# Turning raw rows of x first and normalising them afterwards in a hybrid decoder step

## What is computed

```python
def rms_norm(x, g):
    xf = x.astype(jnp.float32)
    y = xf * lax.rsqrt(jnp.mean(xf * xf, axis=-1, keepdims=True) + NORM_EPS)
    return (y * g.astype(jnp.float32)).astype(x.dtype)

hn   = rms_norm(x, norm_mix_g)              # both groups of tokens
proj = hn @ w_in                            # z, xbc, dt, u5, gates
...                                         # SSD branch, S5 branch from u5, merge
mn   = rms_norm(mem_prompt, norm_mem_kv_g)  # 256 memory tokens
k, v = mn @ w_mem_k, mn @ w_mem_v
...                                         # cross-attention, hierarchical MoE, final norm
```

## Time and profile before

| what | value |
|---|---|
| median of three executions | 1179.93 us (1176.68 to 1180.23) |
| profiled execution, device time | 1180.31 us |
| its span | 1178.6 us |
| PE busy | 980.5 us (83%) |
| DVE busy | 458.9 us (39%) |
| ACT busy | 302.5 us (26%) |
| mean DMA rate | 253 GB/s |
| mean granted TensorE clock | 0.923 of full speed |

### The profile page before, as it was taken

One profiled execution on the slowest core, in us unless ns is written; L12 is line 12 of the kernel. 1 busy time (PEld: TensorE's weight loads), 2 busy tenths in 40 slices (PEclk: granted clock), 3 DMA queues, 4 the chain that ended last, 5 costly groups with the idle time before them and its releaser, 6 DMA issues.

```text
span 1178.6 us, 15892 instructions
## 1 busy us (share of the span) xinstructions
PE 980.5 (83%) x6486; PEld 657.4 (56%) x6486; DVE 458.9 (39%) x854; ACT 302.5 (26%) x608; POOL 53.1 (5%) x78
## 2 busy tenths in 40 slices
PE   3999999999999999999898989666767677755664
PEld 2778567986669999999767953222222222221111
DVE  3998956304667554545554241010011001100113
ACT  4142124225446434534343331000000000000002
POOL 1602200000110000000000000000000000000000
PEclk9999999999999999999999969778888888888888
DMA  9482434013636374523588328999999999999991
GB/s 275 99 202 81 155 117 143 2 40 84 195 92 232 139 290 143 188 85 131 199 305 332 149 107 361 421 421 421 422 420 421 421 422 421 422 421 421 421 421 63
DMA packets 90691, 297.69 MB, mean 253 GB/s; under 512 B 20973, under 2 KB 30921, under 8 KB 65916
## 3 DMA queue, kind: packets, MB, share of 16 engines
q1 hardware_dynamic: 87844, 288.25, 63.8%
q0 software_dynamic: 2256, 7.80, 1.9%
q10 hardware_dynamic: 520, 0.62, 0.2%
HBM read 286.76 MB, written 9.90 MB: 252 GB/s over the span
## 4 chain that ended last, share of the span: by engine, by line
issue 69%; PE 5%; DMA 1%; ACT 0%; POOL 0%; DVE 0%; SPq 0%; POOLq 0%
PE bank L1537 1%; PE bank L1582 1%; DMA ring<-in_state_ssd_dram 1%; PE bank L1265 1%; PE bank L1589 1%; PE bank L1568 0%; PE bank L1546 0%; ACT ops L977 0%; PE bank L1523 0%; PE bank L1593 0%; ACT usplit L969 0%; PE bank L1577 0%; ACT ring L983 0%; POOL out_ssdp_dram L729 0%; DVE ring L2279 0%
## 5 line engine op out<-in xcount | busy, mean ns | idle before, releaser
L1879 PE MATMUL bank<-ring,work 128*32 128x512 f32 x768 | 154.4, 755 | 43.1 <-DMA work<-in_w_exp_up_dram 16.2
L1879 PE MATMUL bank<-work 128*32 128x512 f32 x256 | 115.4, 768 | 37.7 <-DMA ring<-in_w_exp_up_dram 20.9
L1280 PE MATMUL bank<-work,ring 128*128 128x320 f32 (+1 forms) x496 | 131.9, 425 | 0.5 <-DVE work L2048 0.5
L1611 PE MATMUL bank<-ops,usplit 128*128 128x320 f32 x368 | 114.2, 310 | 1.1 <-DVE usplit L2341 1.1
L1612 PE MATMUL bank<-ops,usplit 128*128 128x320 f32 x368 | 114.0, 310 | 0.0
L1613 PE MATMUL bank<-ops,usplit 128*128 128x320 f32 x368 | 114.0, 310 | 0.0
L1280 PEld LDWEIGHTS bank<-work,ring 128*128 128x128 f32 x496 | 94.2, 192 | 33.4 <-issue 2.4
L1894 PE MATMUL bank<-ring,work 128*32 128x512 f32 x384 | 79.2, 786 | 35.9 <-DMA ring<-in_w_exp_down_dram 19.7
L2341 DVE TENSOR_TENSOR usplit<-ring,usplit 128x2048 fp32r<-128x2048 f32 x32 | 73.3, 2291 | 61.8 <-ACT usplit L969 61.5
L1879 PEld LDWEIGHTS bank<-ring,work 128*32 128x32 f32 x768 | 37.9, 134 | 96.2 <-issue 96.2
L969 ACT ACTIVATE usplit<-ring 128x2048 fp32r<-128x2048 f32 x32 | 61.3, 1917 | 51.6 <-PE bank L1613 36.7
(11 more groups left out here) (476 smaller groups left out, 1473.3 us busy)
## 6 DMA issues: line engine op xcount, KB each, us to landing
ring<-in_w_exp_up_dram SPq DMA_DIRECT2D x50, 1024.0 KB, 26.6
ring<-in_w_exp_down_dram SPq DMA_DIRECT2D x48, 1024.0 KB, 26.8
ring<-in_w_exp_gate_dram SPq DMA_DIRECT2D x46, 1024.0 KB, 26.7
ring<-in_w_in_dram SPq DMA_DIRECT2D x11, 2048.0 KB, 8.6
work<-in_w_exp_gate_dram SPq DMA_DIRECT2D x18, 1024.0 KB, 26.1
work<-in_w_exp_down_dram SPq DMA_DIRECT2D x16, 1024.0 KB, 26.5
work<-in_w_exp_up_dram SPq DMA_DIRECT2D x14, 1024.0 KB, 26.4
ring<-in_w_glu_dram SPq DMA_DIRECT2D x4, 2048.0 KB, 8.2
```

The lines of the kernel that those rows point to most:

```text
L1280: ins = nc.tensor.matmul(b[:, 0:N], wv[:, k, P * (m % 4):P * (m % 4 + 1)], src[:, k, 0:N], start=(k == 0), stop=(k == KT - 1))
L1611: nc.tensor.matmul(b[:, 0:T], wh, hi_[:, k], start=(k == 0), stop=False)
L1879: ins = nc.tensor.matmul(psum[part][ES * x:ES * (x + 1), :], xs[i % 2][:, kk, x], wt[x][:, k], start=(kk == 0), stop=(kk == KT - 1))
```

## The change

The rows of x are turned raw, feature block by feature block, without waiting for the root. Each of the eight blocks k goes into a bank of its own (`x0` to `x5` in the ring, 6 and 7 in the free banks); three transposes fill it. The root is spread over the columns by a product of ones with a diagonal matrix (`rx`), which ACT copies to `rsb`. DVE then makes each block of `hnT` with one operation, (block x norm weight) x `rsb`, and PE starts `u50` as soon as its first block is there, taking blocks in the order 0, 1, 2, 3, 4, 6, 7, 5. The sample's sum of squares moves from ACT to DVE. Nine of the small loads stay on ACT's queue under a new semaphore `ld_vec`; four move to SP's queue, ahead of the weight block, and the memory rows move behind that block. The turning of the S5 parameters leaves the job `par` and becomes a job `lam` of its own, between `u50` and `u51`.

```diff
-    j = ["par"]
-    j += [f"x{c}{h}" for c in range(NC) for h in range(2)]
-    j += [f"u5{m}" for m in range(4)]
+    j = ["par"]
+    j += [f"x{k}" for k in range(5)] + ["rx", "x5", "u50", "lam"]
+    j += [f"u5{m}" for m in range(1, 4)]
 ... SP
             sp.dma_start(xt[0:NS, 2, :], ...x_sample...)
-            sp.dma_start(memraw, ...)
+            sp.dma_start(lamrow[0:NST, 0], ...s5_lambda_re...).then_inc(s["ld_par"], 16)
+            sp.dma_start(lamrow[0:NST, 1], ...s5_lambda_im...).then_inc(s["ld_par"], 16)
+            sp.dma_start(lsrow[0:NST], ...s5_log_step...).then_inc(s["ld_par"], 16)
+            sp.dma_start(dd8[0:KT], ...ssd_d...).then_inc(s["ld_par"], 16)
             load_block(0)
+            sp.dma_start(memraw, ...)
 ... ACT
-            (13 small loads on ld_par)
+            (9 small loads on ld_vec)
-            for c in range(NC):
-                R = ROWS[c]
-                act.activation(junk[0:R], xt[0:R, c], ACT.Square, accum_out=ss[0:R, c:c + 1])
+            for c in range(2):
+                act.activation(junk, xt[:, c], ACT.Square, accum_out=ss[:, c:c + 1])
             root(0)
+            got(act, "rx")
+            emptied(act.activation(rsb, bank("rx")[:, 0:T], ACT.Copy), "rx")
             act.wait_ge(s["ld_mem"], 16)
 ... PE
-            pe.wait_ge(s["ld_par"], 16 * 13)
-            pe.wait_ge(s["rows"], 1)
-            (par: vecrow, lamrow, ddrow)
-            for c in range(NC):
-                norm_in(c, "x", c)
-            done(pe, "x21")
-            done(pe, "x20")
-            for m in range(KT):
+            pe.wait_ge(s["ld_vec"], 16 * 9)
+            end(nc.tensor.transpose(b[:, 0:124], vecrow[0:124], ident[0:124, 0:124]), "par")
+            pe.wait_ge(s["ld_x"], 32)
+            for k in range(5):
+                end(rows_of_x(take(f"x{k}"), k), f"x{k}")
+            for k in (6, 7):
+                rows_of_x(psum[k], k)
+            b = take("rx")
+            pe.wait_ge(s["diag"], 1)
+            for c in range(NC):
+                R = ROWS[c]
+                ins = nc.tensor.matmul(b[:, P * c:P * c + R], ones[0:R, :], diag[0:R, c, 0:R], start=True, stop=True)
+            end(ins, "rx")
+            end(rows_of_x(take("x5"), 5), "x5")
+            b = take("u50")
+            have("u50")
+            for n, k in enumerate((0, 1, 2, 3, 4, 6, 7, 5)):
+                if k >= 6:
+                    pe.wait_ge(s["xn"], k - 5)
+                else:
+                    done(pe, f"x{k}")
+                ins = nc.tensor.matmul(b[:, 0:T], blk("u50")[:, k, 0:P], hnT[:, k], start=(n == 0), stop=(n == KT - 1))
+            end(ins, "u50")
+            b = take("lam")
+            pe.wait_ge(s["rows"], 1)
+            (three transposes of lamrow, one of ddrow)
+            for m in range(1, KT):
                 if m == 4:
                     for c in range(2):
-                        norm_in(NC + c, "m", c)
+                        memory_in(c)
                 proj("u5", m, hnT, T)
 ... DVE
+            dve.wait_ge(s["ld_x"], 32)
+            q(TT(junk2[0:NS], xt[0:NS, 2], xt[0:NS, 2], ALU.mult))
+            q(dve.tensor_reduce(ss[0:NS, 2:3], junk2[0:NS], AX.X, ALU.add))
+            (vec from par; step and D rows; s["rows"])
+            dve.wait_ge(s["ss"], 2)
+            root(0)
+            for c in range(NC):
+                ins = TS(diag[:, c], ident[:, :], rs[:, c:c + 1], None, ALU.mult)
+            ins.then_inc(s["diag"], 1)
+            done(dve, "rx")
+            for k in (0, 1, 2, 3, 4, 6, 7, 5):
+                src = bank(f"x{k}") if k < 6 else psum[k]
+                if k == 5:
+                    got(dve, "x5")
+                ins = STT(out=hnT[:, k], in0=src[:, 0:T], scalar=vec[:, V_MIX + k:V_MIX + k + 1], in1=rsb,
+                          op0=ALU.mult, op1=ALU.mult)
+                (emptied, or s["xn"] + 1 for 6 and 7)
+            got(dve, "lam")
+            emptied(dve.tensor_copy(lam[:, :], bank("lam")[:, 0:104]), "lam")
+            done(dve, "lam")
             TS(hglu[:, :], ...).then_inc(s["s5w"], 1)
-            (root(0), then scaled and turned for the three row groups of x)
```

More of the change, by code:

```diff
@@ L218 @@
 SEMS = (
-    "ld_par ld_x ld_mem ld_small ld_s5 ld_b ld_st0 ld_st1 ld_st2 ld_st3 ld_k0 ld_k1 ld_k2 ld_v0 ld_v1 ld_v2 ld_h ld_fin "
+    "ld_vec ld_par ld_x ld_mem ld_small ld_s5 ld_b ld_st0 ld_st1 ld_st2 ld_st3 ld_k0 ld_k1 ld_k2 ld_v0 ld_v1 ld_v2 ld_h ld_fin "
     "dve act pool consts rows ss var rs0 xn s5w s5c s5par bmat btab rtab rot hprev sls ctab kbd xc convout "
@@ L539, in _ @@
             load_block(0)
+            sp.dma_start(memraw, a["mem_prompt"][0].rearrange("(c p) d -> p c d", p=P)).then_inc(s["ld_mem"], 16)
             for ri, name in enumerate(("s5_b_re", "s5_b_im")):
@@ L751, in _ @@
                 k = a[name].shape[1] // P
[L752 to L758, removed]
+                rows(vecrow[at:at + k], a[name][0].rearrange("(k p) -> k p", p=P), "ld_vec")
+            rows(vecrow[V_CW:V_CB], a["conv_w"][0].rearrange("t (k p) -> (t k) p", p=P), "ld_vec")
+            rows(vecrow[V_CB:124], a["conv_b"][0].rearrange("(k p) -> k p", p=P), "ld_vec")
             def sqrt_table():
@@ new lines, in _, with memory_in @@
+            for k in (6, 7):
[7 more added lines that the diff above has]
+            end(rows_of_x(take("x5"), 5), "x5")
+            def memory_in(c):
+                pe.wait_ge(s["xn"], c + 3)
+                for hf in range(2):
+                    b = take(f"m{c}{hf}")
+                    for j in range(4):
+                        ins = tr(b[:, P * j:P * (j + 1)], xn[c][:, P * (4 * hf + j):P * (4 * hf + j + 1)])
+                    end(ins, f"m{c}{hf}")
@@ L1298, in _ @@
             for i in range(3):
[L1299 to L1309, removed]
@@ L2033, in _, with scaled @@
                             dd8[0:KT].unsqueeze(2).to_broadcast([KT, 2, 64])).then_inc(s["rows"], 1)
-            got(dve, "par")
-            dve.tensor_copy(vec[:, :], bank("par")[:, 0:124])
-            emptied(dve.tensor_copy(lam[:, :], bank("par")[:, 128:232]), "par")
             done(dve, "par")
+            dve.wait_ge(s["ss"], 2)
+            root(0)
+            for c in range(NC):
+                ins = TS(diag[:, c], ident[:, :], rs[:, c:c + 1], None, ALU.mult)
[7 more added lines that the diff above has]
+                          op0=ALU.mult, op1=ALU.mult)
+                if k < 6:
+                    emptied(ins, f"x{k}")
+                else:
+                    ins.then_inc(s["xn"], 1)
+            got(dve, "lam")
+            emptied(dve.tensor_copy(lam[:, :], bank("lam")[:, 0:104]), "lam")
+            done(dve, "lam")
             TS(hglu[:, :], vec[:, V_GLU + KT:V_GLU + 2 * KT], 0.5, None, ALU.mult).then_inc(s["s5w"], 1)
[L2039 to L2042, removed]
+            def scaled(c):
+                TS(xn[c], memraw[:, c], rs[:, NC + c:NC + c + 1], None, ALU.mult).then_inc(s["xn"], 1)
             def turned(kind, c, R, dst, v0):
@@ L2101, in _ @@
             q(TT(ci, t1, den, ALU.mult))
-            dve.wait_ge(s["ss"], NC + 2)
+            dve.wait_ge(s["ss"], 4)
             root(1, slice(NC, NC + 2))
             for c in range(2):
-                got(dve, f"x{c + 1}1")
-                scaled(NC + c, memraw[:, c], P)
+                scaled(c)
             dve.wait_ge(s["ld_b"], 32)
```

30 lines of the change are left out of this document (17 added, 13 removed).

## The result

The changed kernel takes 1186.49 us (median of four, 1185.08 to 1190.06) against 1179.29 for the kernel before (four runs). The ratio is 1.0067, with a 95% interval from 1.0046 to 1.0088; the medians differ by 7.2 us, so it is slower. The forecast was 1178.2, with a range up to 1182.2.

The account below looks back on a forecast made before the run. PE was taken as the bound from about 30 us on. u54 would start 3.4 us earlier, less 1.7 for the clock, leaving 1.7: 1180.3 - 1.7 = 1178.6 profiled, 1178.2 for the median, range 1174.5 to 1182.2.

Parts of the forecast that it names:

- PE is the bound behind u54, and a shift at u5 goes through: From about 30 us on PE is the bound; a microsecond won at u5 is worth about a microsecond.
- The memory rows, set by the chain, decide, not the start of u50: Before u54: u50 starts 7.8 us earlier, but u54 cannot pass the memory transposes, whose input hangs on the S5 chain.
- PE's stand before the memory rows: After u53: PE is through at 34.0, the scaled memory rows are ready at 39.6, so it stands 5.6 us.
- The chain gains 2.1 us, not 7.8.: S5 chain on DVE: lam turned after u50, so its first step (L2062) starts at 22.05 instead of 24.11.
- The first fused operation: DVE ahead of u50: loads at 9.6, transposes 4.4, rx 1.0, ACT's copy 0.44, so it starts at 15.9.
- u50 at 6.16 instead of 4.3: PE's u50: 16 instructions at the high clock take 4.3, as PE had worked six microseconds almost without a break.
- the rival in which the slow rate holds: Clock low until u50 is done: u50 takes 7.8, the chain starts 1.7 late, time 1181.9; chance 0.12.
- The table load: ACT ahead of the chain's Exp: 1.3 after the memory squares, bringing ACT to 19.8, 2 us before it is needed.
- The price of the stall: PE's gap before the memory transposes drops the clock to half and costs 1.7, leaving 1.7 of 3.4 at u54.
- The pause there: At hi0: the DRAM trip starts with u57 and moves by 1.7, so the wait of 2.12 us stays.
- The late memory rows (rival): SP's full queue holds their issue: they land at 24.8, chain 4.6 late, u54 5.0, time 1184.9; chance 0.05.
- No change beyond the issue (rival): Start loads: the nine land at 11.5, the chain gains 0.2, time 1180; chance 0.10.

Follow-up runs that it names:

- e1: Changed kernel with the S5 parameters turned before the product that spreads the root; 1177.43 us (10 runs), ratio 0.9998 to the kernel before.
- e3: Changed kernel with the three transposes of block 5 put behind the third block of u50 instead of ahead of u50; 1186.71 us (1 run).
- e10: e7 without its five extra products, so PE stands for about 1 us while ACT copies the root; 1177.34 us (1 run).
- e4: Changed kernel with one dummy Exp on ACT after the squares of the memory rows; 1185.13 us (1 run).
- e5: Changed kernel with six extra 128x128 products on PE while it would wait for the small loads; 1187.01 us (1 run).
- e2: Changed kernel with the 14 transposes of 128 rows first and the 7 of 64 rows after them; 1181.67 us (1 run).
- e7: Changed kernel with the edits of e1, e2 and e3, first Exp ahead of the memory squares, five extra products; 1175.51 us (12 runs), ratio 0.9980.

## Why the prediction was wrong

**PE is the bound behind u54, and a shift at u5 goes through.** Right: u54 5.26 late, hi0 5.97, the landmark at 556 6.0. That u54 is as late as the chain (5.24) is the meeting of two terms. From the start of the scaling of the memory rows to u54 it took 4.62 us in both kernels: before, PE came later than the rows; in the changed kernel, PE waited for them and then turned them at the slow rate. e1, with neither, took 3.22 (39.83 to 43.05). So 1.4 of slack were used up and 1.4 of slow rate came in. In e1 u54 gained 2.19 where the chain gained 0.84.

**The memory rows, set by the chain, decide, not the start of u50.** Right, and it is the core of it. u50 did start earlier (3.55 us, not 7.8), and the kernel got slower all the same. PE's stand before the memory rows, forecast as 5.6 us, was 6.71.

**"The chain gains 2.1 us, not 7.8."** This is the step that failed: the chain lost 5.24. It was forecast at 22.05 and came at 29.35. The 7.3 us are four terms of the sum:

- The first fused operation at 19.18 instead of 15.9: 3.3. The nine loads landed 0.66 later than taken, and the transposes began 0.5 later; they took 6.4 and not 4.4, since I added the times of 128-row and 64-row transposes from rounds where they did not alternate; `rx` took 1.84, since its row came from a stretch at the high rate.
- Block 5 ahead of u50: 1.0 more. Its bank is that of block 0, and PE waits until DVE has emptied it. I did not count the banks, and left out its three transposes altogether. By e3, repairing this alone gives nothing at the chain.
- u50 at 6.16 instead of 4.3: 1.8. I argued that PE had by then worked for six microseconds. It had worked, and it was still slow. The alternating pace is not shown to be the reason: in e10 the transposes were grouped and the rate was low too. This came half true of the rival in which the slow rate holds (7.8 us for u50), priced at 0.12.
- The table load: 1.28, less 0.1 of shorter hand-overs. I placed it ahead of ACT's wait. It came behind the wait; in e4, with a dummy Exp ahead of the wait, it did not stand between `lam` and the chain.

**Which of them turned the sign.** Each is an error towards too early, in a sum of serial terms, and `lam` behind u50 put all of them on the chain. e1 shows it: with the slow transposes, the slow `rx` and the slow u50 all still there, but `lam` off that path, the kernel is level with the one before. I treated the position of `lam` as given and asked only how soon it would come. Against a gain of 2.1, the first term alone (3.3) turns the sign, and so do any two of the other three.

**The price of the stall.** Right in kind, and 0.3 too high. The granted clock fell during PE's stand and was still half when the memory rows were turned (columns as in the earlier trace rows):

```profile
44.00:46.00 2.00, 0.00 (x0) 0.00 (x0) 1.88 (x4) 1.02 (x4) 1.92 (x3) 0.60 1.05 407
46.00:47.00 1.00, 0.00 (x0) 0.00 (x0) 1.00 (x2) 0.00 (x0) 1.00 (x2) 0.50 1.05 393
...
48.00:49.00 1.00, 1.00 (x6) 1.00 (x5) 1.00 (x2) 0.00 (x0) 1.00 (x1) 0.50 0.41 17
```

The 16 transposes took 3.67 against 1.91 before, but part of these 1.76 is not the clock: where PE stands for the rows, the second group waits for its scaling. e1, where PE stood too and the rate held, shows that part. u54 started 2.06 after the first transpose there and 3.47 in the changed kernel: 1.4, where the forecast took 1.7.

**hi0.** The pause there was to stay near 2.1; it was 2.73. The DRAM trip moves with u57, as forecast (the job behind u57 starts at 68.16 against 62.47, 5.7 late). The price of the pause is not the same in every kernel: the first 128 instructions of hi0 took 3.93 in e1, e5 and e10 (pauses of 1.52, 1.97 and 2.06) and 5.27 to 5.48 in the nine others (2.11 to 2.94). In e1 the 1.55 saved there were gone at the landmark, 464.7 us after hi0 against 464.6 before.

**The late memory rows (rival).** The memory rows were in place when ACT came to them at 19.04, so this did not happen. In e2, where ACT came at 15.7, it waited until 17.16. In the changed kernel the long issue on SP's queue fell on `s5_b_im` again (5.63 to 17.42); that a full queue holds it was argued in the prediction and is not tested by any run.

**No change beyond the issue (rival).** The nine loads let PE start at 10.26, against 9.6 taken and 11.5 in this rival, so it did not happen either.

**The size of the whole.** 6.0 us are shown by the rows. The medians differ by 7.2, with an interval of 5.4 to 10.4; whether the remaining 1.2 is scatter or a more frequent second slow stretch behind 556 stays open.

## What to carry to other kernels

Before an early stage is made faster, look for the engine that PE will wait for next, and write down when each input of that engine's chain arrives; an input moved behind a product costs that product's whole length, with every error made in it. Here every error in a sum of serial terms read from other stretches was one towards too early: check the clock level, the neighbouring shapes, the bank each job writes, and what a table load stands behind. A single time did not tell a change of 3 us in this kernel, while the starts of rows in the first 60 us told one of under 1 us.

## What the runs showed of the hardware

- Alternating 128-row and 64-row weight loads hold PE up: 0.91 us for a block of three, against some 0.59 grouped (4.13/7, e10), both at the low rate. The loads show 0.33 us idle once for each change from 128 rows to 64.
- The load of an activation table was issued only when the wait in front of its instruction had ended (27.80 behind `hglu`), and 1.28 us were then on the path; in e4, with a dummy Exp ahead of the wait, it was loaded at 21.52.
- The rate of PE did not rise in the first 13 us of its work, from 10.3 to about 23.5, with alternating transposes, one product of 1.84, a pause of 1.1 and the first six instructions of u50. With the transposes grouped it had risen by about 14 in e2 and e7, but in e10 only during u50. 2.93 us of products from 6.1 on (e5) changed nothing.
- The length of a pause did not alone tell whether the rate fell: behind 2.40 us at the memory rows it held in e10 (16 transposes in 2.22), behind 2.12 us at hi0 it fell in the kernel before (128 instructions in 5.48 instead of 3.93).
- The granted clock reads 1.00 in the windows of the start whatever the rate; only after the first recorded change, as in e2 at 17, does it show the level.
- The Trainium skill, "TensorE: Matmul & The Clock Gate", section "Why this matters for your kernels", asks for sustained work to get the full rate and for no long pause between bursts. The 6.71 us pause agrees (granted clock 0.50 behind it, 16 transposes in 3.67 against 2.23 in e1). The pauses of 2.12 us at hi0 and of 1.11 us in e2 were shorter than the one that rule warns of, and the rate was at half behind them; here the measurement decides. e7 does not test the rule, since its rate was up before the extra products.
